# Where the last head's first gate unit stands among the pooled units of an input projection

## The chip, the cores and the metric

One core of one Trainium2 chip. The metric is the device time of one execution in microseconds (us); lower is better. Where several runs of a kernel are given, the median counts.

## What is computed

One step of a hybrid backbone with one layer (D = 2048) on 640 tokens: 128 context tokens and 512 latent tokens that form an 8 x 64 grid. What matters here is the mixer and what follows it:

```python
def mixer(h, ...):
    z = h @ w_in
    q, k, v, g, a_f, a_b, p = split(z)
    o = gated linear attention over 4 heads of (q, k, v), forward and backward, gates from a_f, a_b
    o = o * rsqrt(mean(o * o)) * gla_norm_g * silu(g)
    pooled = [pool(p[..., 256 * i:256 * i + 256], w) for i, w in enumerate((2, 4, 8, 16))]
    y_pool = einsum(pooled, w_pool) * pool_scale
    return concatenate([o, y_pool]) @ w_out
```

`h` is the layer-normed, modulated input. After the mixer come a residual, a layer norm, a SwiGLU feed-forward block (2048 to 5632 and back), and a second layer norm. A pooled channel is the mean over a window around the token minus the token itself.

## The kernel before

**Number format.** Every large product is made of three matmuls: each f32 operand is split into a rounded high part and a rest (fp32r), and high x high, high x rest and rest x high are added up in PSUM. For weights the high part is made by ScalarE (`split_in`, L1014), the rest by VectorE (`split_rest`, L1414). Two weight units are held at a time, raw and split.

**The input projection.** The columns of `w_in` are cut into 33 units of 128 columns: one for the gate ranks ("a"), four heads of q, k, v, v, g, g, and eight pooled ("p"), two for each window. `unit_plan` (L57) writes down their order, `PLAN`; the weights are laid out in this order in DRAM. A unit has 4 quarters of 24 matmuls (`main_part`, L2107 to L2109), each quarter with both halves of the tokens (320 each), over 4 of 16 k tiles. Its result lies in two of three PSUM banks that are used in turn, so the second half of unit n may begin only when ScalarE has evacuated unit n - 1. Evacuation (`evac`, L1097): q, k, v are copied; a g unit goes through Silu (L1127) into a staging slot and is stored to DRAM by ScalarE's own DMA queue (L1130); a p unit is copied in three pieces into the one padded buffer of the pooling (L1138, L1139, L1142), and waits until VectorE has done with the pooled tile before.

**The order of everything else.** `make_schedule` (L184) puts the attention's steps, the pooling and the modulation's products into the gaps behind quarters, at distances from the positions that units have in `PLAN`. Every engine walks the same list and picks its own items; waits are on semaphores. Of these items:
- ("pool", g, j) is the pooling of one p unit on VectorE (`pool_tile`, L1500, its instructions L1516 to L1549). It stands one quarter into the unit behind its own.
- ("poolmm", g, 0) is the product of two pooled tiles with `w_pool` (TensorE L2148, 16 matmuls). It stands seven quarters behind the beginning of the window's second p unit (eight for the first window), so behind the unit that follows it. ScalarE scales and stores the result (L1197, L1200).
- ("x_load", ...) on SyncE (L774) and ("x_norm", t, 0) on ScalarE (L1212) load and normalise the residual again. They stand at fixed quarters, from 116 on, whatever the plan.
- Head 3's own steps (gate, score, outer, mix, norm) are placed from its k unit.

**The last unit and the output projection.** Unit 32 takes its quarters in the order `KG_ORDER` = (2, 3, 0, 1), and reports each (`last_part`), since the input tiles of the output projection overwrite the columns of x that it has read. SyncE's part after the schedule begins so:

```python
sp.wait_ge(pooled, 8)
for x, k in USES["poolmm", 3, 0]:
    sp.wait_ge(filled[x], k + 1)
load_mix(0)
load_mix(1)
```

`load_mix` (L802, L804) loads one of 16 mixed tiles (128 x 640) from DRAM into one of two buffers, from the third on when the tile two before is split; the first eight are pooled outputs, the others attention outputs with their gates. VectorE makes each into high part and rest (`split_tile`, L1470 and L1471), and multiplies the attention tiles by their gates first. Between them it splits weight units 34, 35 and 36. Behind the loads of the mixed tiles and of the weights up to unit 38 stand the loads of the gate rows (`load_gates`, L813, L816); VectorE prepares the residual with them (L1742 to L1751) and only then splits unit 37.

The output projection (L2304 to L2306) is four column blocks `nb` of four weight units each (33 to 48). Per unit TensorE goes through 5 tiles of tokens with 4 k steps each of 3 matmuls (512 columns). In the first block it waits for the split of each mixed tile:

```python
if nb == 0:
    pe.wait_ge(mix_split, 4 * kg + k + 1)
```

Of the kernel before, what the change touches and what calls it, by code (L numbers as in the profile page):

```python
# [23 lines left out]
P = 128  # L24
# [8 lines left out]
HEADS, DK, DV = 4, 128, 256  # L33
# [17 lines left out]
V_OFF, G_OFF, A_OFF, P_OFF = 1024, 2048, 3072, 3104  # L51
# [5 lines left out]
def unit_plan():  # L57
    plan = [("a", 0, 0, A_OFF)]

    def head(h):  # L60
        return [("q", h, 0, h * DK), ("k", h, 0, KEYW + h * DK),
                ("v", h, 0, V_OFF + h * DV), ("v", h, 1, V_OFF + h * DV + P)]

    def gate(h):
        return [("g", h, 0, G_OFF + h * DV), ("g", h, 1, G_OFF + h * DV + P)]

    plan += head(0)
    for h in range(1, HEADS):
        plan += gate(h - 1) + head(h)
    plan += [("p", j // 2, j % 2, P_OFF + j * P) for j in range(8)]  # L70
    plan += gate(HEADS - 1)
    return plan


PLAN = unit_plan()
assert len(PLAN) == N_IN
KG_ORDER = (2, 3, 0, 1)
# [2447 lines left out]
```

## Time and profile before

| | us |
|---|---|
| median of 3 runs | 2700.77 (2698.55 to 2701.7) |
| the profiled execution | 2699.8 |
| its span in the trace | 2698.0 |
| TensorE busy (matmul) | 2635.9, 98% |
| VectorE busy | 1421.8, 53% |
| ScalarE busy | 897.9, 33% |
| GpSimd busy | 644.7, 24% |

The profile is of one execution. PE is TensorE's matmuls, PEld its weight loads, DVE is VectorE, ACT ScalarE, SP SyncE. A "q" behind an engine marks its DMA issues. L12 is line 12 of the kernel. The times in the span count from its start, which is 1.8 us shorter than the execution's own time. The input projection ends and the output projection begins at about 747 us.

### The profile page before, as it was taken

What the parts mean: (1) busy time and instruction counts of PE and PEld (TensorE: products, weight loads), DVE (VectorE), ACT (ScalarE), POOL (GpSimd) and SP (SyncE); (2) the same over time, 40 slices, a digit from 0 to 9 for tenths busy, and PEclk for the clock granted to TensorE, in tenths of its full rate; (3) what the DMA queues carried; (4) which work ended last, traced back from release to release, by engine and by line L of the source; (5) the groups of instructions that cost most, each with busy time, mean ns of one, the idle gap of its engine ahead of it and who ended that gap; (6) DMA issues with size and microseconds to landing.
All of it is one profiled execution on the core that took longest, in us unless ns stands there. A gap on an engine that the chain in (4) does not pass through costs nothing.

```text
span 2698.0 us, 37412 instructions
## 1 busy us (share of the span) xinstructions
PE 2635.9 (98%) x16040; PEld 2353.1 (87%) x16040; DVE 1421.8 (53%) x1681; ACT 897.9 (33%) x940; POOL 644.7 (24%) x217
## 2 busy tenths in 40 slices
PE   5999999999999999999999999999999999999997
PEld 3787878797988879999999999999999888888886
DVE  5323332356575458555565545554556444444578
ACT  4333333333311154333333333333333333333243
POOL 0000000000000001434443444344433333333440
PEclk8999999999999999999999999999999999999999
DMA  9775757423463142333233223322334646454586
GB/s 378 281 267 208 275 201 272 161 78 107 178 219 125 61 157 84 106 109 98 84 109 109 92 90 109 109 89 92 109 109 148 239 175 214 175 215 168 193 275 226
DMA packets 182024, 438.11 MB, mean 162 GB/s; under 512 B 10060, under 2 KB 30932, under 8 KB 175716
## 3 DMA queue, kind: packets, MB, share of 16 engines
q1 hardware_dynamic: 179556, 430.48, 45.8%
q10 hardware_dynamic: 2304, 5.24, 0.5%
q8 instruction: 127, 2.08, 0.3%
q14 instruction: 37, 0.30, 0.0%
HBM read 401.83 MB, written 33.85 MB: 161 GB/s over the span
## 4 chain that ended last, share of the span: by engine, by line
PE 73%; POOL 8%; DVE 7%; DMA 6%; issue 3%; ACT 2%; SPq 0%; POOLq 0%; ACTq 0%; DVEq 0%
PE ps L2357 7%; PE ps L2358 7%; PE ps L2359 7%; PE ps L2434 7%; PE ps L2435 7%; PE ps L2436 7%; PE ps L2107 5%; PE ps L2109 5%; PE ps L2108 5%; DMA raw_w<-w_gu_b 4%; PE ps L2087 3%; PE ps L2306 3%; PE ps L2305 3%; PE ps L2304 3%; POOL raw_w L981 2%
## 5 line engine op out<-in xcount | busy, mean ns | idle before, releaser
L1703 DVE TENSOR_TENSOR w_lo<-raw_w,w_hi 128x1024 fp32r<-128x1024 f32 x264 | 336.3, 1275 | 296.8 <-ACT w_hi L1247 294.0
L1247 ACT ACTIVATE w_hi<-raw_w 128x1024 fp32r<-128x1024 f32 x264 | 270.0, 1054 | 599.5 <-POOL raw_w L987 378.6
L2357 PE MATMUL ps<-x_hi,w_hi 128*128 128x320 f32 x1408 | 435.8, 310 | 3.6 <-DVE w_lo L1703 2.0
L2359 PE MATMUL ps<-x_hi,w_lo 128*128 128x320 f32 x1408 | 435.1, 309 | 0.0
L2358 PE MATMUL ps<-x_lo,w_hi 128*128 128x320 f32 x1408 | 435.0, 309 | 0.0
L978 POOL TENSOR_TENSOR low<-raw_w 128x1024 f32<-128x1024 f32 x41 | 104.2, 2543 | 1085.0 <-DMA raw_w<-w_gu_b 1031.4
L1848 DVE TENSOR_TENSOR x_lo<-low,x_hi 128x2560 fp32r<-128x2560 f32 (+2 forms) x55 | 223.4, 4062 | 261.4 <-ACT x_hi L1340 261.4
L2434 PE MATMUL ps<-w_hi,x_hi 128*128 128x512 f32 x880 | 342.8, 390 | 2.0 <-POOL w_lo L993 0.8
L2435 PE MATMUL ps<-w_lo,x_hi 128*128 128x512 f32 x880 | 342.4, 389 | 0.0
L2436 PE MATMUL ps<-w_hi,x_lo 128*128 128x512 f32 x880 | 342.3, 389 | 0.0
L2357 PE MATMUL ps<-low_r,w_hi 128*128 128x320 f32 x1072 | 331.9, 310 | 0.8 <-DVE low_r L1789 0.7
L2359 PE MATMUL ps<-low_r,w_lo 128*128 128x320 f32 x1072 | 331.2, 309 | 0.0
L2358 PE MATMUL ps<-low_r,w_hi 128*128 128x320 f32 x1072 | 331.2, 309 | 0.0
L2107 PE MATMUL ps<-x_hi,w_hi 128*128 128x320 f32 x1024 | 324.5, 317 | 5.0 <-ACT low L1142 3.2
L2109 PE MATMUL ps<-x_hi,w_lo 128*128 128x320 f32 x1024 | 318.0, 311 | 0.0
L2108 PE MATMUL ps<-x_lo,w_hi 128*128 128x320 f32 x1024 | 317.9, 310 | 0.0
L993 POOL TENSOR_TENSOR w_lo<-raw_w,w_hi 128x2048 fp32r<-128x2048 f32 x44 | 203.9, 4633 | 355.8 <-ACT w_hi L1349 355.8
L2357 PEld LDWEIGHTS ps<-x_hi,w_hi 128*128 128x128 f32 x1408 | 264.3, 188 | 4.7 <-DVE w_lo L1703 2.7
L2358 PEld LDWEIGHTS ps<-x_lo,w_hi 128*128 128x128 f32 x1408 | 264.3, 188 | 0.0
L2359 PEld LDWEIGHTS ps<-x_hi,w_lo 128*128 128x128 f32 x1408 | 264.3, 188 | 0.0
L1414 DVE TENSOR_TENSOR w_lo<-raw_w,w_hi 128x2048 fp32r<-128x2048 f32 x48 | 110.0, 2291 | 255.8 <-ACT w_hi L1014 255.7
L2107 PEld LDWEIGHTS ps<-x_hi,w_hi 128*128 128x128 f32 x1024 | 193.6, 189 | 32.9 <-issue 26.1
(241 smaller groups left out, 4262.3 us busy)
## 6 DMA issues: line engine op xcount, KB each, us to landing
raw_w<-w_gu_b SPq DMA_DIRECT2D x180, 512.0 KB, 5.6
low<-w_ada SPq DMA_DIRECT2D x68, 1024.0 KB, 6.9
raw_w<-w_down SPq DMA_DIRECT2D x50, 1024.0 KB, 5.1
low<-hidden_scratch SPq DMA_DIRECT2D x33, 1280.0 KB, 6.1
raw_w<-w_in_b SPq DMA_DIRECT2D x33, 1024.0 KB, 9.1
x_raw<-w_ada SPq DMA_DIRECT2D x25, 1024.0 KB, 14.4
raw_w<-w_out SPq DMA_DIRECT2D x16, 1024.0 KB, 5.1
hidden_scratch<-high SPq DMA_DIRECT2D x44, 320.0 KB, 5.8
```

The lines of the kernel that those rows point to most:

```text
L1247: nc.scalar.activation(weight(0, w), src, ACT.Copy).then_inc(prod_hi, 1)
L1703: nc.vector.tensor_tensor(weight(1, n), src, weight(0, n).bitcast(F32), ALU.subtract).then_inc(prod_split, 1)
L1848: nc.vector.tensor_tensor(hid_slot(x_lo, j), hid_raw(j), hid_slot(x_hi, j).bitcast(F32), ALU.subtract).then_inc(hid_split, 1)
L2107: mm(out, wh, xh, start=first, stop=False)
L2108: mm(out, wh, xl, start=False, stop=False)
L2109: ins = mm(out, wl, xh, start=False, stop=last)
L2357: mm(out, wh, version(v, 0, k), start=first and k == 0, stop=False)
L2358: mm(out, wh, version(v, 1, k), start=False, stop=False)
L2359: ins = mm(out, wl, version(v, 0, k), start=False, stop=last and k == HK - 1)
L2434: mm(ps[:, (i + 7) % 8, :], xh, rh, start=begin, stop=False)
L2435: mm(ps[:, (i + 7) % 8, :], xh, rl, start=False, stop=False)
L2436: ins = mm(ps[:, (i + 7) % 8, :], xl, rh, start=False, stop=end)
```

## The change

The eight pooled units stood together in places 23 to 30, with the last head's two gate units in places 31 and 32. Now the first of these gate units stands in place 26, behind three pooled units; the other five pooled units take places 27 to 31, each one later than before; the second gate unit stays in place 32. All that `make_schedule` puts at a distance from a pooled unit moves with it: pooled tiles 3 to 7 and the products of windows 1 to 3 (for the last window, the product now stands behind unit 32). Weights in DRAM follow the plan. No instruction's form changes.

```diff
     for h in range(1, HEADS):
         plan += gate(h - 1) + head(h)
-    plan += [("p", j // 2, j % 2, P_OFF + j * P) for j in range(8)]
-    plan += gate(HEADS - 1)
-    return plan
+    pools = [("p", j // 2, j % 2, P_OFF + j * P) for j in range(8)]
+    between, after = gate(HEADS - 1)
+    return plan + pools[:3] + [between] + pools[3:] + [after]
```

## Rows read from the trace of the kernel before

**Rows 1.** Page, busy time by engine: busy us (share) xinstructions.
```profile
PE 2635.9 (98%) x16040; PEld 2353.1 (87%) x16040; DVE 1421.8 (53%) x1681; ACT 897.9 (33%) x940; POOL 644.7 (24%) x217
```

**Rows 2.** Waits of TensorE, 560 to 1080 us: total, times, longest us.
```profile
PE ps L2107 <- ACT low L1142: 3.2, 1, 3.2
...
PE ps L2148 <- DVE low L1599: 1.2, 1, 1.2
```

**Rows 3.** Timeline of TensorE: start, length us, instruction, count, [idle before <- releaser].
```profile
617.71 0.42 PE L2107 MATMUL ps<-x_hi,w_hi 128*128 128x320 f32 x1 [3.16 <-ACT low L1142]
...
618.83 0.47 PE L2107 MATMUL ps<-x_hi,w_hi 128*128 128x320 f32 x1
...
619.10 0.47 PE L2108 MATMUL ps<-x_lo,w_hi 128*128 128x320 f32 x1
...
623.72 4.56 PE L2148 MATMUL ps<-low 128*128 128x512 f32 x16 [1.17 <-DVE low L1599]
...
728.10 4.59 PE L2148 MATMUL ps<-low 128*128 128x512 f32 x16 [0.20 <-DVE low L1549]
...
732.44 0.39 PE L2107 MATMUL ps<-x_hi,w_hi 128*128 128x320 f32 x1
...
746.61 0.39 PE L2304 MATMUL ps<-w_hi,x_hi 128*128 128x512 f32 x1
```

**Rows 4.** Windows of all engines; the column PEclk is the granted clock.
```profile
core 0: us, PE busy (x) PEld busy (x) DVE busy (x) ACT busy (x) POOL busy (x), PEclk, DMA share, GB/s
...
618.00:620.00 2.00, 2.00 (x11) 2.00 (x11) 0.51 (x1) 1.46 (x1) 0.00 (x0) 0.63 0.03 8
...
747.00:801.00 54.00, 54.00 (x239) 44.70 (x239) 38.62 (x52) 8.25 (x6) 0.00 (x0) 1.00 0.71 239
```

**Rows 5.** Timeline of ScalarE, 640 to 775 us.
```profile
640.99 0.28 ACT L1138 ACTIVATE low<-ps 128x128 f32<-128x128 f32 x1 [11.82 <-PE ps L2109]
...
713.85 0.28 ACT L1138 ACTIVATE low<-ps 128x128 f32<-128x128 f32 x1 [9.35 <-PE ps L2109]
...
727.93 0.77 ACT L1127 ACTIVATE low<-ps 128x320 f32<-128x320 f32 x2 [6.19 <-PE ps L2109]
...
729.15 1.91 ACT L1014 ACTIVATE w_hi<-raw_w 128x2048 fp32r<-128x2048 f32 x1 [0.46 <-ACT low L1127]
...
760.49 1.92 ACT L1014 ACTIVATE w_hi<-raw_w 128x2048 fp32r<-128x2048 f32 x1 [10.55 <-PE ps L2306]
...
774.09 1.92 ACT L1014 ACTIVATE w_hi<-raw_w 128x2048 fp32r<-128x2048 f32 x1 [11.68 <-PE ps L2306]
```

**Rows 6.** Timeline of VectorE, 718 to 812 us.
```profile
718.72 1.31 DVE L1516 TENSOR_TENSOR low<-low 128x143 f32<-128x143 f32 x4
...
727.35 0.69 DVE L1549 TENSOR_TENSOR low<-low 128x512 f32<-128x512 f32 x1
...
736.25 0.49 DVE L1470 CAST x_hi<-low 128x640 fp32r<-128x640 f32 x1 [2.86 <-PE ps L2109]
...
743.21 0.82 DVE L1471 TENSOR_TENSOR x_lo<-low,x_hi 128x640 fp32r<-128x640 f32 x1
...
749.98 2.29 DVE L1414 TENSOR_TENSOR w_lo<-raw_w,w_hi 128x2048 fp32r<-128x2048 f32 x1 [0.96 <-ACT w_hi L1014]
...
783.75 0.83 DVE L1471 TENSOR_TENSOR x_lo<-low,x_hi 128x640 fp32r<-128x640 f32 x1
...
790.36 0.69 DVE L1742 TENSOR_TENSOR low<-low 128x512 f32<-128x512 f32 x1 [5.14 <-DMA low<-rows]
...
797.95 2.29 DVE L1414 TENSOR_TENSOR w_lo<-raw_w,w_hi 128x2048 fp32r<-128x2048 f32 x1
...
810.43 2.27 DVE L1414 TENSOR_TENSOR w_lo<-raw_w,w_hi 128x2048 fp32r<-128x2048 f32 x1
```

**Rows 7.** Timeline of SyncE; last, the landing of the loads of line L802.
```profile
677.14 3.67 SPq L774 DMA_DIRECT2D low<-x_all  x5
...
732.85 11.53 SPq L802 DMA_DIRECT2D low<-mixed_scratch  x6
...
DMA to landing us min/median/max: 2.7/3.6/4.1
```

## The prediction

> **What bounds the kernel now.** I read the page first: TensorE is busy for 98% of the span [rows 1]. So a change of order, which adds and removes no matmul, can only gain where TensorE idles, and loses wherever it makes TensorE idle anew. Then the waits of TensorE, from 560 to 1080 us, which show how little there is to win near the change: 3.2 us before one matmul of the projection (waiting for ScalarE's evacuation, L1142), and 1.2 us before the first pooled product (L2148) [rows 2]. The timeline places the longer one and shows 0.2 us before the last product. The 3.2 us end at 617.71, in main unit 26, where TensorE has done the first half of the tokens and wants the bank that unit 25's evacuation frees; the 0.2 us end at 728.10 [rows 3]. Between unit 32's last matmul and the output projection's first there is no gap. Last the windows: from 747 to 801 us, where the first quarter of the output projection runs, TensorE is busy all the time at the full clock [rows 4].
>
> Both larger waits lie ahead of anything that the change moves. Unit 25 is the third pooled unit in both orders; its evacuation is behind the second decay gate of head 3 on ScalarE, whose place doesn't change. Only 0.2 us (0.01%) can be won on TensorE, unless something else shifts. The question is what the new order costs, and the place to look is the end of the projection.
>
> **Part 1, units 26 to 31.** Unit 26 becomes a gate unit. Its 96 matmuls are the same. ScalarE evacuates it with Silu and then issues one 320 KB store from its own queue. It needs a table load first, and such a load is issued ahead of the wait; ScalarE is idle for 11.82 us before it evacuates unit 26 [rows 5], which covers it. The store and its wait stand before the split of the next weights: in unit 31 that split starts 1.2 us after the evacuation (727.93, 729.15 [rows 5]). It costs nothing, because those weights are used a unit later; if that cover went, it would be at most the 1.2 us. Pooled tiles 3 to 7 (counted from 0) come one unit later with their weight loads on SyncE. Their conditions shift with them: each tile still has a unit (14.1 us, from 713.85 to 727.93 between two evacuations [rows 5]), and the longest tile takes 9.3 us of VectorE, from 718.72 to 728.04 [rows 6]. On SyncE the reload of x (5 MB, first issue at 677.14 [rows 7]) keeps its place in the order but now has the second pooled product, a unit later than before, ahead of it. It slips by less than a unit; its user is a normalisation on ScalarE that nobody waits for in this stage, and the weight load behind it is wanted after unit 30, at about 709. I take zero, between 0 and 2 us (the slip over what two units leave). POOL issues nothing here.
>
> **Part 2, the last pooled product.** This is what costs. Before, it stands after unit 31 and is followed by unit 32's 14.17 us of matmuls (732.44 to 746.61), under which the output projection's inputs are made: SyncE waits for the product, then loads 16 tiles through two buffers, and VectorE splits each. After, the last pooled unit is 31, so the product stands after unit 32, with nothing of the projection left behind it. Step by step:
> - Unit 31 ends at 727.9 as before (its evacuation starts at 727.93). Unit 32 follows at once and ends at about 727.9 + 14.2 = 742.1.
> - The last pooled tile is ready 14.2 us after the evacuation before it begins (713.85 to 728.04 [rows 5, 6]), so at 727.93 + 14.2 = 742.1: no wait, or 0.2 us.
> - The product takes 4.59 us [rows 3] and ends at 746.8. TensorE has done exactly what it had done before at that time.
> - SyncE's first tile load was issued at 732.85, right behind the product [rows 7]; now at about 746.95, 14.1 us later.
> - VectorE's first cast, 736.25, had waited for TensorE's quarter of unit 32 rather than for the load [rows 6], so a part of the 3.4 us from the issue falls away: between 0 (load as late as the cast) and 0.7 us (the fastest landing of these loads, 2.7 us [rows 7]). I take 0.2. The chain of tiles is 13.9 us late.
> - The fourth split ended at 743.21 + 0.82 = 744.0, now at 757.9. The first row of tokens needs all four for its four k steps. TensorE has 20 such steps in a weight unit of 13.60 us [rows 5], 0.68 us each. Three can run in the waits, 17 x 0.68 = 11.6 us remain: the first unit ends at 769.5, not 760.2. **First cost 9.3 us.**
> - Then I follow VectorE. In its chain it had waited 0.96 us for ScalarE at 749.98; ScalarE is now early, so from here the lag is 12.9 us. Units 34 to 36 of the weights and the tiles behind them arrive before TensorE, which is itself 9.3 us late: the sixteenth tile, done at 783.75 + 0.83 = 784.6 [rows 6], comes at 797.5, and its step at 746.61 + 3 x 13.60 + 3 x 0.68 + 9.3 = 798.8. No cost, with 1 us to spare.
> - The rows of gates are loaded behind a weight load that waits for one of these splits. VectorE waited 5.14 us for them until 790.36, and only after 7.6 us on them splits the weights of unit 37 (797.95 + 2.29 = 800.24) [rows 6]. TensorE wanted those at 746.61 + 4 x 13.60 = 801.0. The slack is 0.8 us now. The split moves to 800.24 + 12.9 = 813.1, TensorE comes at 801.0 + 9.3 = 810.3. **Second cost 2.8 us**, together 12.1 us.
> - The next split, begun at 810.43, ended at 812.7 and was wanted at 814.6; its lag is 12.9 against 12.1, so it holds. Later splits wait for ScalarE, which follows TensorE.
>
> After that stage everything hangs on TensorE's end, and its waits there are on VectorE and ScalarE, which lag by the same amount. Nothing is given back. Sum: 2699.8 + 12.1 = 2711.9 us against the profiled execution (span 2698.0 and 1.8 around it). The median shown is 2700.8, 1.0 above it, so 2712.9.
>
> **The clock.** In the 3.2 us wait at 614.6 TensorE went idle, and the windows show the granted clock at 0.63 from 618 to 620: it had fallen from 2.4 to 1.2 GHz, and matmul starts are 0.27 us apart at 618.83 and 619.10, where unit 32 has 14.17 / 96 = 0.15 [rows 3, 4]. The new wait (746.8 to 751.5, then three more with single steps between) is longer, so a fall is likely. At the low level a step costs 0.68 x 0.27 / 0.15 = 1.22 us, 0.54 more. Six of the 17 steps at that level add 3.2 us; but the second cost leaves 2.8 us in which this is hidden, so 0.4 shows. I take 0 and let the range carry the rest. If all 17 ran low, it would be 9.2, of which 6.4 show.
>
> The Trainium skill's page "TensorE: Matmul & The Clock Gate" (Part 1, the HAM clock gate) speaks against the change too: an idle array drops to half rate and regains the full rate only after sustained work. The trace agrees, by the 0.63 above. By that rule alone the first unit would start at half rate and the sum would be nearer the clock rival below.
>
> **The rivals.**
> - **A, the forecast**: the gate rows and split 37 decide; 2713, own range 2710 to 2715. For it: the slack of 0.8 us. Chance 0.60.
> - **B, only the first wait counts**: the rows land sooner, since the reload's traffic is further away, and the second cost vanishes: 2700.8 + 9.3 = 2710. Against it: VectorE's wait for them is 5.14 us of landing in a chain of dependent issues. 0.12.
> - **C, the clock**: half rate for 9 or more of the dense steps adds 4.9 us or more to the first cost: 9.3 + 4.9 = 14.2, 2715; with all 17 low 18.5, 2719. For it: four waits in 12 us. Against: the low stretch at 618 gave way again before the pooled product at 623.72, whose 16 matmuls took their usual 4.6 us. 0.23.
> - **D, not slower**: the split chain of the first row is ready before TensorE asks. It has its place at 746.61: the fourth split ended at 744.0 and its step wants it at 748.7, a slack of 4.6 us. So the product would have to be filled by 737.3, in the middle of unit 32. TensorE's order puts it behind that unit, so this needs a lag of 4.6 us or less where I work out 13.9. Then the time is 2700.8 less the 0.2 us, 2700.6. Likewise, a slower start could be paid back if the 3.2 and 1.2 us waits vanished with what the clock cost there (some 12 matmuls at 0.12 us, 1.5 us): 5.9 us, still under 9.3. 0.04 for no change or better.
> - The last 0.01 is for a wait that I don't see.
>
> **How the numbers follow.** The time is that of A. The range takes in B's 2710, with 0.5 us below it for loads that land at their fastest, and C up to 2717.5, leaving out its tail and D. A measurement of this kernel can tell about 0.2% (5.4 us) from no change. A, B and C are all above: slower 0.96, same 0.03, faster 0.01.
>
> **What would show it.** TensorE: the product directly behind unit 32 at about 742 to 747, then a wait of about 5 us on a split of x (L1471), three shorter ones, and one near 810 us on a weight split (L1414). SyncE: the first tile load at about 747. VectorE: the cast that follows it at 750. TensorE's waits of 3.2 and 1.2 us at 614 and 623 unchanged. The windows from 747 to 762 with a clock below 1. The prediction is wrong if the tile loads start before unit 32 ends, if the wait near 810 us is missing (B), if a wait appears between 640 and 742 us, or if a lag of 12 us at 815 us is no longer there at the end.

## The result and the profile after

The changed kernel takes 2712.45 us in the median of 6 runs (2709.69 to 2715.15), the kernel before 2700.65 (6 runs, 2698.55 to 2702.39). The ratio is 1.0043 (95% interval 1.0033 to 1.0053): slower, by 11.8 us in the medians. Forecast were 2713.0 and slower.

The profiled execution took 2715.15 us (span 2713.4), 15.4 us of span more than the one before. Three parts make it, and only one of them is the change. The first evacuation of a pooled unit (unit 23, far ahead of any moved unit) shows how much later this execution ran already. ScalarE's split of unit 39 begins when TensorE has done unit 37, the fifth weight unit of the output projection, and shows the lag behind the first column block. Timeline of ScalarE, kernel before:

```profile
577.76 0.28 ACT L1138 ACTIVATE low<-ps 128x128 f32<-128x128 f32 x1 [2.81 <-PE ps L2109]
...
814.89 1.92 ACT L1014 ACTIVATE w_hi<-raw_w 128x2048 fp32r<-128x2048 f32 x1 [11.68 <-PE ps L2306]
```

The same view of the changed kernel, with the split of unit 35 between, which begins when the first weight unit of the output projection is done (before: 760.49 [rows 5]):

```profile
579.30 0.28 ACT L1138 ACTIVATE low<-ps 128x128 f32<-128x128 f32 x1 [2.81 <-PE ps L2109]
...
773.48 1.92 ACT L1014 ACTIVATE w_hi<-raw_w 128x2048 fp32r<-128x2048 f32 x1 [24.23 <-PE ps L2306]
...
828.51 1.92 ACT L1014 ACTIVATE w_hi<-raw_w 128x2048 fp32r<-128x2048 f32 x1 [12.31 <-PE ps L2306]
```

579.30 - 577.76 = 1.5 us is a late start of this execution. With it taken off, the lag is 773.48 - 760.49 - 1.54 = 11.45 us after the first weight unit and 828.51 - 814.89 - 1.54 = 12.1 us after the fifth. From here on I call these two numbers the first and the second lag. Of the 1.8 us that are left of the 15.4, 1.4 arise in a later stage, to which I come below.

The waits of TensorE, 560 to 1095 us (total, times, longest), have two new rows, and the two that lay ahead of the change are what they were [rows 2]:

```profile
PE ps L2304 <- DVE x_lo L1471: 7.2, 2, 5.9
PE ps L2107 <- ACT low L1142: 3.2, 1, 3.2
...
PE ps L2148 <- DVE low L1599: 1.2, 1, 1.2
...
PE ps L2304 <- DVE w_lo L1414: 0.3, 1, 0.3
PE ps L2148 <- DVE low L1549: 0.2, 1, 0.2
```

The timeline of TensorE shows them in order: the last pooled product (before at 728.10 [rows 3], now behind unit 32), and the first, third and fourth step of the output projection:

```profile
743.76 4.59 PE L2148 MATMUL ps<-low 128*128 128x512 f32 x16 [0.20 <-DVE low L1549]
...
754.22 0.77 PE L2304 MATMUL ps<-w_hi,x_hi 128*128 128x512 f32 x1 [5.87 <-DVE x_lo L1471]
...
758.43 0.80 PE L2304 MATMUL ps<-w_hi,x_hi 128*128 128x512 f32 x1 [1.31 <-DVE x_lo L1471]
...
760.14 0.80 PE L2304 MATMUL ps<-w_hi,x_hi 128*128 128x512 f32 x1
...
763.70 0.39 PE L2304 MATMUL ps<-w_hi,x_hi 128*128 128x512 f32 x1
```

The last row is the seventh step. Such a matmul took 0.39 us at 746.61 [rows 3] and takes 0.77 and 0.80 here, and 0.39 again in the seventh step. Of the three shorter waits that the prediction wanted, the trace has one, 1.3 us before the third step: the steps had become so slow that TensorE came to the second and fourth split about when they were done. The windows say why the steps were slow. Their sixth group (PEclk) is the granted clock:

```profile
core 0: us, PE busy (x) PEld busy (x) DVE busy (x) ACT busy (x) POOL busy (x), PEclk, DMA share, GB/s
640.00:741.00 101.00, 101.00 (x660) 92.60 (x659) 59.29 (x131) 34.65 (x39) 0.00 (x0) 1.00 0.38 137
...
754.00:763.00 9.00, 7.41 (x16) 4.85 (x17) 5.26 (x9) 0.00 (x0) 0.00 (x0) 0.50 0.59 166
970.00:1000.00 30.00, 29.16 (x136) 21.97 (x135) 24.60 (x49) 21.26 (x29) 0.00 (x0) 0.83 0.20 73
```

From 640 to 741 us, over units 27 to 31, TensorE isn't idle at all, and its only waits in unit 26 are the two old ones. Then it waits, the clock falls to 1.2 GHz and is there for the whole of 754 to 763 us, some 10 us in all. The last row is the layer norm's stage, in which this execution ran a third of the time at 1.2 GHz and the one before at full clock. A weight split of ScalarE's at 1047.19 us before comes at 1062.23 here, 15.04 later, where the split of unit 39 came 13.62 later: 1.4 us were lost between them.

VectorE and SyncE, which make the inputs: the first tile load and the reload of x (before 732.85 and 677.14 [rows 7]),

```profile
683.43 2.76 SPq L774 DMA_DIRECT2D low<-x_all  x5
...
748.52 11.91 SPq L802 DMA_DIRECT2D low<-mixed_scratch  x6
```

and on VectorE the first cast, the fourth split, the work on the gate rows and unit 37's split (before 736.25, 743.21, 790.36 and 797.95 [rows 6]):

```profile
752.72 0.49 DVE L1470 CAST x_hi<-low 128x640 fp32r<-128x640 f32 x1 [9.02 <-DMA low<-mixed_scratch]
...
759.26 0.83 DVE L1471 TENSOR_TENSOR x_lo<-low,x_hi 128x640 fp32r<-128x640 f32 x1
...
804.58 1.42 DVE L1742 TENSOR_TENSOR low<-low 128x512 f32<-128x512 f32 x2 [6.43 <-DMA low<-rows]
...
812.17 2.29 DVE L1414 TENSOR_TENSOR w_lo<-raw_w,w_hi 128x2048 fp32r<-128x2048 f32 x1
```

### The profile page after: what moved, and what is told of

Read it like the earlier page. It is cut to its first block, busy times and chain, and to the rows that moved or that the text cites. A ratio compares the mean times of both kernels' runs of the same rounds, so it can differ in the third digit from the quotient of the medians.

```text
span 2713.4 us, 37413 instructions
## 1 busy us (share of the span) xinstructions
PE 2645.9 (98%) x16040; PEld 2357.5 (87%) x16040; DVE 1443.0 (53%) x1681; ACT 898.5 (33%) x941; POOL 640.4 (24%) x217
## 4 chain that ended last, share of the span: by engine, by line
PE 79%; DVE 6%; DMA 6%; POOL 4%; ACT 2%; issue 2%; SPq 0%; POOLq 0%; ACTq 0%; DVEq 0%
PE ps L2357 10%; PE ps L2358 10%; PE ps L2359 10%; PE ps L2434 7%; PE ps L2436 7%; PE ps L2435 7%; PE ps L2107 5%; PE ps L2109 5%; PE ps L2108 5%; PE ps L2087 3%; DMA raw_w<-w_gu_b 2%; PE ps L2304 2%; PE ps L2305 2%; PE ps L2306 2%; PE ps L2148 2%
## 5 line engine op out<-in xcount | busy, mean ns | idle before, releaser
L1703 DVE TENSOR_TENSOR w_lo<-raw_w,w_hi 128x1024 fp32r<-128x1024 f32 x264 | 346.9, 1314 | 298.7 <-ACT w_hi L1247 296.2
```

The lines of the kernel that those rows point to most:

```text
L1703: nc.vector.tensor_tensor(weight(1, n), src, weight(0, n).bitcast(F32), ALU.subtract).then_inc(prod_split, 1)
```

## The experiments

All are timed against the kernel before on the same chip, with 5 or more runs each. Lags are taken from one profiled execution each, as above (first: ScalarE's split of unit 35, behind the first weight unit; second: its split of unit 39, behind the fifth; the late start of each execution taken off). A profiled execution isn't always near its kernel's median: that of rows_early was the shortest of five (2711.15 us), that of inputs_ahead the longest of eleven (2704.66), that of rows_early_full_busy 2715.47.

| kernel | median, us | ratio (95% interval) | first lag | second lag |
|---|---|---|---|---|
| the change | 2712.45 | 1.0043 (1.0033 to 1.0053) | 11.5 | 12.1 |
| late_product | 2710.81 | 1.0041 (1.0029 to 1.0054) | 10.7 | 10.8 |
| inputs_ahead | 2701.92 | 1.0007 (0.9998 to 1.0016) | 0.0 | 2.4 |
| inputs_split_first | 2698.77 | 0.9995 (0.9986 to 1.0004) | 0.0 | 0.0 |
| inputs_rows_ahead | 2702.68 | 1.0011 (1.0002 to 1.0020) | 0.0 | 2.8 |
| rows_early | 2714.11 | 1.0050 (1.0038 to 1.0063) | 10.6 | 12.1 |
| kept_busy | 2711.97 | 1.0044 (1.0031 to 1.0056) | 10.7 | 12.0 |
| full_busy | 2711.06 | 1.0039 (1.0026 to 1.0052) | 9.6 | 11.7 |
| rows_early_full_busy | 2712.68 | 1.0048 (1.0034 to 1.0062) | 9.6 | 14.8 |
| split_first | 2709.61 | 1.0034 (1.0021 to 1.0047) | 10.9 | 10.9 |
| split_first_full_busy | 2709.53 | 1.0036 (1.0022 to 1.0050) | 9.5 | 9.5 |
| second_place | 2700.17 | 0.9999 (0.9990 to 1.0007) | -3.4 | -1.0 |
| second_place_split_first | 2695.21 | 0.9982 (0.9973 to 0.9991) | -3.4 | -3.4 |

### Which half of the change costs: late_product and inputs_ahead

My theory was that the place of the last pooled product against unit 32 is the whole cost; the rival was the gate unit and the five later tiles themselves. late_product leaves the order of the kernel before and moves only this product:

```diff
-        put(where["p", g, 1], 7, ("poolmm", g, 0))
+        put(where["p", g, 1], 11 if g == 3 else 7, ("poolmm", g, 0))
```

> The order of the units is that of the kernel before; only the last pooled product (TensorE L2148) is put behind unit 32 instead of behind unit 31. If my theory holds (the place of this product against unit 32 is the whole cost), the time is that of the changed kernel: 12 us above the kernel before, 2710 to 2715, with a wait of 5 to 6 us on the first split of x (L1471) at about 747 us. Rival: the gate unit in place 26 and the later pooled tiles carry the cost (ScalarE's Silu, stores, the reload of x behind the products); then this kernel is within 2 us of the kernel before.

Measured: 1.0041, on the side of the theory; the rival's "within 2 us" is out. Its waits of TensorE, 640 to 960 us:

```profile
PE ps L2304 <- DVE x_lo L1471: 7.4, 3, 5.4
```

There is no wait before unit 37 in it: TensorE wants that unit's split at 801.0 + 10.7 = 811.7 us, and the split ends at 809.82 + 2.29 - 0.46 = 811.65 (0.46 is this execution's late start), 1.3 us sooner than in the change. So here the first wait and the low clock (0.79 over 747 to 763 us) make the whole lag.

inputs_ahead is the other half: the changed order, with the tie between the last product and the output projection's inputs cut. The first eight tiles are pooled outputs and need no gates; three idle pieces of SBUF hold them (`high` from 0 and from 1600, and the row buffer of the even windows).

```diff
+    def y_tile(i):
+        return (high[:, 0:T], high[:, 1600:1600 + T], lo(L_RC, T))[i % 3]
...
-            if i >= 2:
-                sp.wait_ge(mix_split, i - 1)
+            if i < 8:
+                if i >= 3:
+                    sp.wait_ge(mix_split, i - 2)
+            else:
+                if i == 8:
+                    sp.wait_ge(pooled, 8)
+                    for x, k in USES["poolmm", 3, 0]:
+                        sp.wait_ge(filled[x], k + 1)
+                if i >= 10:
+                    sp.wait_ge(mix_split, i - 1)
...
-        sp.wait_ge(pooled, 8)
-        for x, k in USES["poolmm", 3, 0]:
-            sp.wait_ge(filled[x], k + 1)
+        sp.wait_ge(scores_summed, HEADS)
+        sp.wait_ge(row_out, 16 * 8)
         load_mix(0)
         load_mix(1)
+        sp.wait_ge(pooled, 6)
+        load_mix(2)
```

> The changed kernel, but the eight pooled input tiles of the output projection go to three buffers that the pooling doesn't use, and SyncE waits for the last pooled product only before the ninth tile. The first three are loaded during unit 32 and the first is split as soon as VectorE has the last pooled tile done (about 742 us). My theory: the first cost and the fall of the clock go, and the second cost with them: 2700 to 2702.5, no wait over 1 us between 640 and 950 us. Rival (the first part of the change costs something by itself): what stays above 2701 is its price, up to 12.

The first lag is gone entirely. The second isn't, against my expectation that it would go with the first; the median, 1.9 us above the kernel before's in the same rounds, is inside the expected range. The waits of TensorE, 640 to 960 us, name it:

```profile
PE ps L2324 <- DVE w_lo L1431: 2.1, 1, 2.1
PE ps L2168 <- DVE low L1566: 0.2, 1, 0.2
```

L1431 is `split_rest` there, and the wait stands ahead of unit 37. The mixed attention tiles, which still go through two buffers behind the last product, and the gate rows behind them are late here too. This is the limit of the prediction's second cost, without the first; the split is less late than in the change, so its 2.1 us isn't that cost's size there. inputs_split_first takes it away. It splits unit 37 ahead of the gate rows, in the time in which VectorE waits for them:

```diff
         for nb in range(4):
+            if nb == 0:
+                split_rest(N_IN + 4)
             dve.wait_ge(gate_in[nb % 2], 80 * (nb // 2 + 1))
...
-            for kg in range(2 if nb == 0 else 0, 3):
+            for kg in range(3 if nb == 0 else 0, 3):
```

> The kernel inputs_ahead with unit 37's split ahead of the gate rows. Its 2.1 us wait before unit 37 goes, and loading the rows isn't moved. Theory: the end of the output projection is within 1 us of the kernel before, the time 2700 to 2701.5. Rival (part 1 of the change costs something): 2702 or more, without a wait of TensorE's between 640 and 950 us that explains it.

Measured: 0.9995, both lags 0.0, and one row of waits between 640 and 960 us, the 0.2 us one. The median, 2698.77, is 1.2 below what I expected at least, inside what a measurement can tell. So the moved gate unit and the later tiles cost nothing that these runs show: by the interval, at most 0.04%, 1.1 us.

### The clock and the gate rows: two limits that stand in for each other

In the changed kernel the wait before unit 37 was 0.3 us, not 2.8: TensorE came to it late, because the first unit ended 2.1 us later than forecast, mostly by the low clock. If so, removing one of the two alone should give little back. kept_busy fills the longest wait with 24 matmuls that nobody reads (PSUM bank 3, overwritten later):

```diff
         pe.wait_ge(zin_evac, N_IN - 1)
 
+        pe.wait_ge(split_done, N_IN + 1)
+        for f in range(24):
+            mm(ps[:, 3, :], w_hi[:, 0, 0:P], w_hi[:, 0, 0:512], start=True, stop=True)
```

> The changed kernel, with 24 matmuls more (512 columns each, into a PSUM bank that is overwritten later) between the last pooled product and the output projection, inside the wait of 5.9 us. Theory: TensorE is not idle, the granted clock stays at 1.00 until 754 us or later and the first unit of the output projection ends up to 2 us earlier; the rows' split then decides and a wait of 1 to 2.5 us stands before unit 37; the time is within 1 us of the changed kernel. Rival (the clock is a cost by itself): 2 us below it, 2710.3, and no longer wait before unit 37.

It kept the full clock through the long wait, but TensorE then waited 2.1 and 0.7 us at the third and fourth step, and the clock fell for a stretch after all (0.89 over 747 to 763 us). A wait of 1.0 us came before unit 37, and the time didn't move. full_busy fills those waits too:

```diff
                         ins = mm(ps[:, i % 7, :], xl, rh, start=False, stop=end)
+                        for f in range({1: 8, 2: 2}.get(k, 0) if u == N_IN and t == 0 else 0):
+                            mm(ps[:, 3, :], w_hi[:, 0, 0:P], w_hi[:, 0, 0:512], start=True, stop=True)
```

> The kernel kept_busy with 8 more matmuls in the wait behind the second step and 2 in the one behind the third, so that TensorE is never idle between the last pooled product and the dense steps. Theory: the granted clock stays at 1.00 from 743 to 800 us; the first unit of the output projection then ends about 3 us sooner than with the low clock; but the gate rows' split of unit 37 stands where it stood, so a wait of 2.5 to 3 us comes before unit 37, and the time is that of the changed kernel (2711 to 2713). Rival (the clock costs by itself): 3 us less and no such wait.

Its window and its waits of TensorE (640 to 960 us):

```profile
743.00:800.00 57.00, 56.09 (x243) 44.35 (x242) 34.47 (x47) 9.16 (x7) 0.00 (x0) 1.00 0.73 248
```

```profile
PE ps L2308 <- DVE w_lo L1414: 1.8, 1, 1.8
PE ps L2308 <- DVE x_lo L1471: 0.9, 3, 0.4
```

The first lag falls by 1.9 us to 9.6, which is the first cost without the clock. Of the 1.9, 1.4 are the clock and 0.5 a fourth split that ended sooner (757.47 + 0.83 - 0.22 = 758.1, in the change 758.6; 0.22 is this execution's late start). They come back as a wait of 1.8 us for the split of unit 37. That wait is shorter than the 2.5 to 3 us I had written. The time, 1.0039, isn't told apart from the change's 1.0043.

rows_early goes at the other limit. It moves the loads of the gate rows from behind mixed tile 15 (counted from 0) to behind tile 9:

```diff
-            if i == 5:
+            if i == 3:
                 for x in range(2):
                     sp.wait_ge(spilled[x], 16 * n_out[x])
                     sp.wait_ge(drained[x], FILLS[x])
                 sp.wait_ge(row_out, 16 * 8)
                 load_gates(0)
+            if i == 5:
                 sp.wait_ge(mix_split, KT)
```

> The changed kernel, with the gate rows of the first column block loaded behind mixed tile 9 instead of behind tile 15. In the changed kernel's trace TensorE came to unit 37 only 0.3 us before its split, because the low clock had made the first unit 2.2 us longer. Theory as it stands after that trace: the first cost and the clock decide, the rows hardly: 0 to 1 us below the changed kernel, 2711.5 to 2712.5, the 0.3 us wait gone. Rival (the sum as I forecast it, where the rows' split decides): 2.8 us below it, 2709.7.

The wait before unit 37 went, but nothing was won: the median is 1.7 us above the change's, with intervals that overlap. The rival's 2.8 us gain is refuted, and my own "0 to 1 below" wasn't met either. The edit brings a cost that I hadn't put in. Its lag grows from 10.6 to 12.1 us between the first and the fifth unit, with a wait of 1.2 us on a mixed tile. rows_early_full_busy shows the same thing larger:

> The edits of full_busy and of rows_early together: neither the low clock nor the rows' split. Theory: what is left is the first cost alone, 9.3 us: 2709 to 2710.5, 2 to 3 us below full_busy, with no wait before unit 37. Rival (the two don't stand in for each other): both single edits left the time where it was, and so does this one, 2712.

Missed: the median is 2712.68, 2.2 us above the range, and the second lag is 14.8 us, the largest of all (in an execution 2.8 us above the median). The waits of TensorE (640 to 960 us) and VectorE at the eleventh tile:

```profile
PE ps L2309 <- DVE x_lo L1472: 4.3, 4, 1.8
```

```profile
786.38 0.83 DVE L1695 TENSOR_TENSOR low<-low 128x640 f32<-128x640 f32 x1 [7.21 <-DMA low<-silu_g_scratch]
```

VectorE waits 7.2 us for one tile behind five loads of gate rows and a weight load. The slowest landing of a tile's gates (L804) is 9.3 us here, against 5.4 in the change, and the slowest of a mixed tile (L802) in rows_early 9.3 us, against 4.7. This pair didn't test what I wanted, since the edit puts a third limit in the place of the second. The same shows in inputs_rows_ahead:

> The kernel inputs_ahead, with the gate rows loaded behind mixed tile 9. In inputs_ahead the only wait left between 640 and 950 us was 2.1 us before unit 37, on the split that stands behind the rows. Theory: it goes, and the time is that of the kernel before, 2699.5 to 2701, in spite of the moved gate unit. Rival (the moved unit and tiles cost something of their own): 1.5 to 2 us above the kernel before, as inputs_ahead.

The 2.1 us wait went and two waits on mixed tiles, 2.0 us together, came; 1.0011, as its rival has it, but by a wait that the edit made.

split_first and split_first_full_busy take away the second limit without moving a load (the edit of inputs_split_first on the changed kernel):

> The changed kernel, with VectorE splitting unit 37's weights ahead of the gate rows (while it waits for them) instead of behind the 7.6 us of work on them. Nothing is loaded earlier, so no load of mixed tiles is delayed as in rows_early. Theory: the second cost is gone, but with the low clock in the first unit it was only 0.3 us: 0 to 1 us below the changed kernel, 2711.5 to 2712.5, no wait before unit 37.

> The edits of split_first and of full_busy together. full_busy kept the clock at 1.00 and lost the gain again in a wait of 1.8 us before unit 37; here that wait can't arise. Theory (the low clock and the rows' split stand in for each other): only the first cost is left, 9.3 us, 2709.3 to 2710.3 and 1.5 to 2.5 us below full_busy (2711.1), no wait before unit 37. Rival: there is a third limit near 12 us (mixed tiles 13 to 16): a wait on a split of x (L1471) stands at 785 to 800 us and the time stays at 2711 to 2712.

With both gone, first and second lag are the same 9.5 us. This is the first cost as forecast (9.3), alone, up to unit 37. Behind it the third limit shows, though not the rival's: the next split, unit 38's, ends 0.6 us after TensorE wants it. TensorE's waits, 750 to 960 us, have it:

```profile
PE ps L2310 <- DVE w_lo L1414: 0.5, 1, 0.5
```

The forecast had this split hold against a lag of 12.1; with TensorE only 9.5 late it doesn't, and the lag is 10.2 us from there on. The medians are 9.6 us above the kernel before here and 10.8 in full_busy, with ratios (1.0036 and 1.0039) whose intervals overlap, so the gain in time isn't shown; the lags show it. split_first alone came to 2709.61, lower than my 2711.5 to 2712.5. Its execution had a first wait of 4.7 us where the change's had 5.87, by an earlier landing of the first tile, and no wait before unit 37; the interval overlaps the change's. How much of the 2.8 us between the medians is the edit stays open (2.1 us, with each kernel's own runs of the kernel before taken off).

### A version that beats both: second_place and second_place_split_first

TensorE's two old waits (3.2 and 1.2 us) both lie in unit 26. ScalarE can't evacuate unit 25 before head 3's second cumulative step, which VectorE reaches late because the second pooled tile stands ahead of the gate (it comes to the gate at 606.51 us in the kernel before, and at 602.97 in second_place, whose execution started 0.8 us late). A gate unit in place 25 needs no pooled tile to be evacuated, so the tile may go behind:

```diff
-    return plan + pools[:3] + [between] + pools[3:] + [after]
+    return plan + pools[:2] + [between] + pools[2:] + [after]
...
-    put(where["p", 0, 1], 8, ("poolmm", 0, 0))
+    put(where["p", 0, 1], 9, ("poolmm", 0, 0))
...
-        put(where["p", j // 2, j % 2], (5, 3)[j] if j < 2 else 4, ("pool", j // 2, j % 2))
+        put(where["p", j // 2, j % 2], (5, 6)[j] if j < 2 else 4, ("pool", j // 2, j % 2))
```

second_place has this on top of inputs_rows_ahead:

> inputs_rows_ahead, with the gate unit one place earlier (place 25, behind two pooled units), the second pooled tile behind head 3's second cumulative step instead of ahead of its gate, and the first pooled product one quarter later. Theory: TensorE's waits of 3.2 us (unit 26, behind ScalarE's evacuation) and 1.2 us (first pooled product) and the low clock behind the first go: 4 to 6 us below inputs_rows_ahead, 2695 to 2697. Rival: the wait of 3.2 us has another cause than the pooled tile that stands ahead of the gate on VectorE (the chain of the gate itself is too long for a unit), and 3 us of it stay: 2699 to 2700.

Measured: 2700.17 us, near the rival's time but not by its cause. The first lag is -3.4 us, the 3.2 us wait is gone, and so is the low clock behind it. The early rows then cost 1.8 us in waits on tiles. It is 2.5 us below inputs_rows_ahead, not 4 to 6. second_place_split_first has the edit of split_first in place of the early rows:

> The kernel second_place without the early gate rows and with unit 37's split ahead of them. second_place lost TensorE's 3.2 us wait and the low clock behind it, but had two new waits on mixed tiles (0.6 and 1.2 us) behind the early rows. Theory: these go, 2696.5 to 2699, the fastest so far and 1 to 3 us below the kernel before. Rival: the waits on mixed tiles come from the order of the tiles' loads themselves; then 2700.

Measured: 2695.21 us, ratio 0.9982 (0.9973 to 0.9991), faster than both kernels. Its waits of TensorE, 560 to 960 us, and the window over the old wait:

```profile
PE ps L2170 <- DVE low L1616: 1.1, 1, 1.1
PE ps L2129 <- ACT low L1159: 0.7, 1, 0.7
...
PE ps L2170 <- DVE low L1566: 0.2, 1, 0.2
PE ps L2129 <- ACT low L1144: 0.2, 1, 0.2
```

```profile
605.00:625.00 20.00, 18.73 (x127) 16.08 (x127) 14.63 (x28) 8.55 (x11) 0.00 (x0) 1.00 0.23 86
```

Of the 4.7 us below the kernel before, the lags show 3.4; where the rest arises stays open. The wait of the first pooled product wasn't removed by the quarter that I gave it: it is 1.1 us, behind the same mask of the scores (L1599 before, L1616 here), which VectorE now reaches behind the second pooled tile and a weight split. A wait of 0.7 us behind a pooled unit's evacuation (L1159) is new. With the gate unit in place 26, as in the change, both old waits stayed in every kernel that I traced. second_place_split_first differs from inputs_split_first by this edit alone, and their intervals (0.9973 to 0.9991 and 0.9986 to 1.0004) overlap a little.

## Why the prediction was right, step by step

- **No gain ahead of the change**: right. Both waits are unchanged (3.2 and 1.2 us), and TensorE is busy for all of 640 to 741 us.
- **Part 1 costs nothing**: right within 1.1 us, by inputs_split_first. The reload of x moved by 683.43 - 677.14 - 1.54 = 4.8 us, less than a unit, and nobody waited.
- **The product's place**: right. It begins at 743.76, less the late start 742.2 (forecast 742.1 or 0.2 later), takes 4.59 us, and SyncE's first load follows at 748.52 - 1.54 = 747.0 (forecast 746.95).
- **First cost 9.3 us**: the term was right for the full clock, 9.6 and 9.5 us where TensorE was kept busy. In the changed kernel the first lag is 11.45: 0.7 us of the 2.1 above the forecast are a later fourth split, the rest is the clock. The cast came at 752.72 - 1.54 = 751.2, where I had 736.25 + 13.9 = 750.2, but the fourth split ended at 760.09 - 1.54 = 758.6, 0.7 late against 757.9.
- **Second cost 2.8 us**: the mechanism was right and its size in the change wrong, 0.3 us. Where TensorE came to unit 37 without the low clock, it was a wait of 1.8 us (full_busy); the same limit gave 2.1 us in inputs_ahead. The split itself ended at 812.17 + 2.29 - 1.54 = 812.9 (forecast 813.1).
- **The clock, taken at 0**: the term that was mis-sized. The fall was called likely and its cost said to be hidden in the slack of 2.8 us. From the fourth step to the seventh TensorE took 763.70 - 760.14 = 3.56 us, where three steps at full clock take 3 x 0.68 = 2.04: the clock cost 1.5 us, and 9.3 + 0.7 + 1.5 is the first lag. It was less than the 3.2 us that six low steps would have cost, as most of the low stretch lay in the waits and in the first three steps: fewer than three of the 17 dense steps ran low. The late split and the clock together took the wait before unit 37 down to 0.3 us and its share of the lag to 12.1 - 11.45 = 0.6 (a lag grows by 0.3 more than the wait in full_busy and inputs_ahead too, 2.1 for 1.8 and 2.4 for 2.1). So the sum came out at 12.1 and the trace shows 12.1, though by 11.45 + 0.6 and not by 9.3 + 2.8. When unit 37 can begin is set by the later of two limits, forecast 2.8 us apart. The later one, the split, was forecast to 0.2 us, and the error in the other was hidden behind it. That it was hidden whole is luck: 0.6 us more, and it would have shown, and in late_product the split came 1.3 us sooner than in the change.
- **The rivals**: B (only the first wait) is out for the change, where unit 37 waited for its split (0.3 us, 1.0 in kept_busy, 1.8 in full_busy). In late_product the split was just in time, so between these two kernels the second cost is within what executions differ by. C was half right: the clock fell for some 10 us, but over fewer than three dense steps and not nine, and at the end it costs about what the slack could hide. D is out: the fourth split was 758.6 - 744.0 = 14.6 us late, not under 4.6.
- Nothing was given back later, as forecast: the medians differ by 11.8 us. Of the clock, the Trainium skill's rule in "TensorE: Matmul & The Clock Gate" (Part 1), that an idle array loses the full rate, held in each execution that had the long wait. These are the change, late_product, rows_early and split_first, with 0.68 to 0.79 over 747 to 763 us.

## What to carry to other kernels

When a unit of work moves, look at what is tied to the last of its kind by a distance. Here five tiles one place later were free, and one product that slipped behind the last unit took away the cover of the next stage's whole input chain. When TensorE is late by one chain, follow the other chains too and compare ends, since the time follows the latest one, and an experiment on a single one may show nothing. To free a limit that stands behind a wait for a load, move work into the wait rather than the load forward: the earlier load delayed others that were closer to the edge.

## What the runs showed of the hardware

- Short waits were enough to bring the clock down after a busy stretch: in kept_busy TensorE was idle for 2.1 and 0.7 us with one step between, and it still fell for a while, to an average of 0.89 over 747 to 763 us.
- The same stage doesn't always run at the same clock. Over 950 to 1020 us, around the layer norm's stage, nine of the 14 profiled executions kept 1.00 and five had 0.93, the change, inputs_ahead, inputs_rows_ahead, kept_busy and second_place. In the kernel before and in the change the wait that starts the stage is the same 0.6 us; behind it one kept the clock and the other lost it. The slow matmuls also took up waits: 0.7 and 1.7 us before became 0.2 in the change. It cost 1.4 us there, in a kernel whose runs spread over 5.
- With five broadcast loads of gate rows and a weight load moved in front of tile loads on one queue, the slowest mixed tile's landing went from 4.7 us (the change) to 9.3 (rows_early) and 7.3 (rows_early_full_busy).
